# A two-block Trainium2 kernel: the second block's output gate, branch gates and branch projections in pairs of column tiles, seven half-size products for each pair

## What is computed

```python
proj = h @ w_in
(q_att, c_kv, q_idx, k_idx, w_idx, qkv, a, b, z, gates) = jnp.split(proj, SPLITS, axis=-1)
y_att = dsa_attention(...)
o = chunk_gated_delta_rule(...)                       # 8 heads of 128
y_dn = rms_norm_2(o, norm_g) * silu(z)
gates = sigmoid(gates)
g_att, g_dn = gates[..., :1024], gates[..., 1024:]
merged = g_att * (y_att @ w_br_att) + g_dn * (y_dn @ w_br_dn)
return merged @ w_out
```

## Time and profile before

| | us |
|---|---|
| median of 3 runs | 2307.83 |
| lowest and highest | 2305.79, 2315.35 |
| the profiled execution, its own time | 2306.49 |
| its span in the profile | 2304.8 |
| PE busy | 2222.1 |
| DVE busy | 901.3 |
| ACT busy | 469.4 |
| POOL busy | 114.3 |
| mean granted TensorE clock | 0.984 |

### The profile page before, as it was taken

The page is one execution under the profiler, slowest core; times in us unless marked ns, Lnnn a source line. Parts: engine busy times, 40 slices in busy tenths (PEclk is TensorE's granted clock), DMA queues, the critical chain, the costliest instruction groups (busy, mean ns, idle before and its releaser), DMA issues.

```text
span 2304.8 us, 22750 instructions
## 1 busy us (share of the span) xinstructions
PE 2222.1 (96%) x8731; PEld 1247.6 (54%) x8731; DVE 901.3 (39%) x1693; ACT 469.4 (20%) x984; POOL 114.3 (5%) x210
## 2 busy tenths in 40 slices
PE   8999999999999999999899999999999899999997
PEld 3447444468888444544656569444445544454443
DVE  3685532168887101185525755110015311111115
ACT  2134020112222001124535445100000100000002
POOL 0000000000000000000011000000000100000001
PEclk9999999999999999999999999999999899999999
DMA  4245222325555222112121110622241699999997
GB/s 158 73 162 194 73 73 73 119 88 178 184 172 183 55 73 91 57 55 81 42 78 55 58 52 1 249 105 79 73 145 55 258 428 427 428 425 427 427 428 300
DMA packets 45390, 385.23 MB, mean 167 GB/s; under 512 B 7066, under 2 KB 7194, under 8 KB 18650
## 3 DMA queue, kind: packets, MB, share of 16 engines
q1 hardware_dynamic: 30816, 317.39, 34.6%
q0 software_dynamic: 14176, 49.06, 6.2%
q10 hardware_dynamic: 289, 17.30, 2.2%
HBM read 369.54 MB, written 35.68 MB: 176 GB/s over the span
## 4 chain that ended last, share of the span: by engine, by line
PE 86%; DVE 5%; DMA 3%; issue 3%; ACT 1%; DVEq 1%; POOL 0%; SPq 0%; ACTq 0%; POOLq 0%
PE banks L591 22%; PE banks L1351 20%; PE banks L493 11%; PE banks L2605 8%; PE banks L2732 5%; PE banks L2618 4%; PE banks L1467 3%; PE banks L1590 2%; DMA arena<-in_experts 2%; DMA ring<-in_experts 1%; PE banks L600 1%; PE banks L646 1%; PE banks L662 1%; DVE arena L2072 1%; PE banks L653 1%
## 5 line engine op out<-in xcount | busy, mean ns | idle before, releaser
L1351 PE MATMUL banks<-arena,ring 128*128 128x512 f32 x1296 | 563.9, 595 | 0.0
L591 PE MATMUL banks<-arena,ring 128*128 128x512 f32 x1184 | 514.4, 595 | 5.9 <-DVE arena L1063 3.3
L1351 PEld LDWEIGHTS banks<-arena,ring 128*128 128x128 f32 x1296 | 245.7, 191 | 302.0 <-issue 300.5
L591 PEld LDWEIGHTS banks<-arena,ring 128*128 128x128 f32 x1184 | 225.7, 191 | 291.2 <-issue 283.2
L493 PE MATMUL banks<-ring 128*128 128x256 f32 x672 | 161.0, 389 | 8.0 <-DVE ring L463 3.9
L1657 ACT ACTIVATE arena<-banks 128x512 f32<-128x512 f32 (+4 forms) x151 | 78.5, 532 | 392.2 <-PE banks L1351 320.4
L493 PEld LDWEIGHTS banks<-ring 128*128 128x128 f32 x672 | 130.7, 195 | 27.8 <-DVE ring L463 4.3
L2732 PEld LDWEIGHTS banks<-arena 128*128 128x128 f32 x1024 | 121.0, 198 | 30.2 <-issue 28.9
L2732 PE MATMUL banks<-arena 128*128 128x128 f32 x1024 | 126.9, 284 | 5.7 <-issue 4.5
L2605 PE MATMUL banks<-ring,arena 128*64 128x512 f32 x528 | 120.1, 603 | 4.6 <-DMA ring<-in_experts 3.1
L493 PE MATMUL banks<-arena,ring 128*128 128x256 f32 x504 | 119.6, 380 | 0.0
(11 more groups left out here) (372 smaller groups left out, 1990.1 us busy)
## 6 DMA issues: line engine op xcount, KB each, us to landing
ring<-in_stream SPq DMA_DIRECT2D x105, 1024.0 KB, 4.8
arena<-in_experts SPq DMA_DIRECT2D x52, 2048.0 KB, 24.3
ring<-in_experts SPq DMA_DIRECT2D x44, 2048.0 KB, 21.9
arena<-in_w_adaT POOLq DMA_DIRECT2D x48, 512.0 KB, 4.7
expert_results<-arena POOLq DMA_DIRECT2D x60, 128.0 KB, 7.4
arena<-modulation_rows POOLq DMA_DIRECT2D x5, 512.0 KB, 9.8
arena<-in_xT SPq DMA_DIRECT2D x2, 1024.0 KB, 6.3
first_result<-arena POOLq DMA_DIRECT2D x4, 512.0 KB, 2.9
```

Source lines behind the costliest of these rows:

```text
L591: m = pe.matmul(bank, c.weight(at + k), rhs(k), start=k == 0, stop=k == tiles - 1)
L1351: m = pe.matmul(bank, c.weight(at + k), rhs(k), start=k == 0, stop=k == tiles - 1)
```

## The change

The 40 gemms `z`, `ga`, `gd`, `ba` and `bd` become 20 pairs in `pairs_pe`: four of `z`, eight of (`ga` t, `gd` t), four of `ba`, four of `bd`. `Halves` now carries its rows, its row sums and the count of `moving_sums` that it waits for, since three sets of rows are in use (h, the turned attention result, the delta result). The sums of h go to the fourth quarter of `ring` at the start of the second block's DVE program; those of the attention result to `BA_` during pair 9; those of the delta result to the fourth quarter of `ring` during pair 13. `moving_sums` counts each of its four instructions. Delta results are scaled in pairs 0 to 3 and turned, two jobs at a time, behind the closing of pairs 4 to 7. `ga` is kept in the `V_` region and `gd` in `BA_` + 4096, all eight tiles of each. Two of the three loads of `first_experts` (parts 0 and 1 of expert 0, whose places are the third and fourth quarter of `ring`) move behind the last `bd`. POOL's load of the first block's result waits for the last `ba` in place of the last `oT`. The `rank` job of the router gets bank 6.

```diff
-def moving_sums(c, v, rows):
+def moving_sums(c, v, rows, mixed):
...
+    v.tensor_tensor(t1, b12, b11, ALU.subtract).then_inc(c.sem("moving_sums"), 1)
+    v.tensor_tensor(t3, b22, b12, ALU.subtract).then_inc(c.sem("moving_sums"), 1)
...
 def pair_second(c, pe, h):
     pe.wait_ge(c.sem("pair_seeded"), h.n + 1)
+    pe.wait_ge(c.sem("moving_sums"), h.sums + 3)
...
 def pair_closes(c, pe, h):
     pe.wait_ge(c.sem("pair_lower"), h.n + 1)
+    pe.wait_ge(c.sem("moving_sums"), h.sums + 4)
...
+MIX_PAIRS = [(("z", 2 * i), ("z", 2 * i + 1)) for i in range(DH // 2)] \
+    + [(("ga", i), ("gd", i)) for i in range(DT)] \
+    + [((n, 2 * i), (n, 2 * i + 1)) for n in ("ba", "bd") for i in range(DT // 2)]
+SCALES_O, TURNS_O, MIXES_Y, MIXES_O = range(0, 4), range(4, 8), 9, 13
+
+def turns_o(j):
+    return (2 * (j - TURNS_O[0]), 2 * (j - TURNS_O[0]) + 1) if j in TURNS_O else ()
+
+def mix_pairs(c, h_sums):
+    h, yT, q = (c.view(at, DT, S) for at in (H_, K_, Q_))
+    sources = {"z": (h, c.mixed(), h_sums), "ga": (h, c.mixed(), h_sums),
+               "ba": (yT, c.mixed(BA_), h_sums + 4), "bd": (q, c.mixed(), h_sums + 8)}
+    return [Halves(c, a, b, *sources[a[0]]) for a, b in MIX_PAIRS]
...
 # plan_second
+    p.rotation((6, 7), (0, 2, 4))
+    for j, ((a, i), (b, k)) in enumerate(MIX_PAIRS):
+        p.pair((a, i, MIXERS[a][0]), (b, k, MIXERS[b][0]), [...])
+        for t in turns_o(j):
+            p.job("oT", t, "dve")
...
 # second_pe
-    for hd in range(DH):
-        gemm("z", hd, lambda k: h[:, k, :], DT)
-    for b in range(2 * TT):
-        pe.wait_ge(c.sem("o_scaled"), b + 1)
-        each("oT", b, lambda o, j, hd: pe.transpose(o, q[:, hd, ts(b)], c.ident[:, :]))
-    for t in range(DT):
-        gemm("ga", t, ...)
-        gemm("ba", t, ...)
-        gemm("gd", t, ...)
-        gemm("bd", t, ...)
+    def turn_o(j):
+        if j == MIXES_Y:
+            pe.wait_ge(c.sem("y_back"), 16)
+        for b in turns_o(j):
+            pe.wait_ge(c.sem("o_scaled"), b + 1)
+            each("oT", b, lambda o, j, hd: pe.transpose(o, q[:, hd, ts(b)], c.ident[:, :]))
+    pairs_pe(c, pe, mix_pairs(c, SECOND_SUMS), closed=turn_o)
...
 # second_act
+    pair_seeds(c, a, mixes[0])
     a.wait_ge(c.sem("powers"), 4)
     a.activation(sm[:, SO_S:SO_S + 32], sm[:, SO_S:SO_S + 32], ACT.Sqrt).then_inc(sem("powers_back"), 1)
+    for j, h in enumerate(mixes):
+        if j:
+            activated(mixes[j - 1].second)
+        if j + 1 < len(mixes):
+            pair_seeds(c, a, mixes[j + 1])
+        activated(h.first)
...
 # second_dve, at its start
+    v.wait_ge(c.sem("h"), DT)
+    moving_sums(c, v, h, c.mixed())
...
 # second_dve, behind the delta rule
+    weight_sums(c, v, mixes[0].n)
+    weight_sums(c, v, mixes[1].n)
     v.wait_ge(*c.put_away("o", 2 * TT - 1))
     v.scalar_tensor_tensor(power, ...).then_inc(sem("powers"), 1)
...
+    for j, p in enumerate(mixes):
+        pair_upper(c, v, p)
+        if j:
+            gated(mixes[j - 1].second)
+            for b in turns_o(j - 1):
+                turned_o(b)
+        pair_lower(c, v, p)
+        gated(p.first)
+        if j + 2 < len(mixes):
+            weight_sums(c, v, mixes[j + 2].n)
+        if j == SCALES_O[0]:
+            v.wait_ge(c.sem("powers_back"), 4)
+            v.reciprocal(power, power)
+            v.drain()
+        if j in SCALES_O:
+            scale_o(2 * j)
+            scale_o(2 * j + 1)
+        if j == MIXES_Y:
+            v.drain()
+            v.wait_ge(c.sem("y_back"), 16)
+            moving_sums(c, v, c.view(K_, DT, S), c.mixed(BA_))
+        if j == MIXES_O:
+            v.drain()
+            v.wait_ge(*c.finished("gd", DT - 1))
+            moving_sums(c, v, q, c.mixed())
+    gated(mixes[-1].second)
...
 # second_pool
-    g.wait_ge(*c.put_away("oT", 2 * TT - 1))
+    g.wait_ge(*c.finished("ba", DT - 1))
     g.dma_start(c.view(XTOK_, TT, D), c.x_spill).then_inc(c.sem("x_back"), 16)
...
 def first_experts(c, sp):
     load_expert(c, sp, 1, 1)
-    for i in range(2):
-        load_expert(c, sp, 0, i)
...
 # experts_sp
     sp.wait_ge(*c.finished("ba", DT - 1))
     load(2, 0)
+    sp.wait_ge(*c.finished("bd", DT - 1))
+    load(0, 0)
+    load(0, 1)
     sp.wait_ge(*c.put_away("bd", DT - 1))
     load(1, 2)
```

More of the change, by code:

```diff
@@ L47 @@
 MEAN_AT = 3
+SECOND_SUMS = 4
 class Plan:
@@ L478, with __init__ @@
 class Halves:
-    def __init__(self, c, first, second):
+    def __init__(self, c, first, second, rows, mixed, sums):
         self.c, self.first, self.second = c, first, second
@@ L484, in __init__ @@
         self.at = c.plan.pair_at[self.n]
+        self.rows, self.mixed, self.sums = rows, mixed, sums
         a, b = c.bank(*first), c.bank(*second)
@@ L492, in pair_product, with pair_opens @@
     for k in range(4):
-        m = pe.matmul(out, weights[:, k * P:(k + 1) * P], moving(k), start=first and k == 0, stop=k == 3,
+        m = pe.matmul(out, weights[:, k * P:(k + 1) * P], moving[:, k, :], start=first and k == 0, stop=k == 3,
                       skip_group_check=True)
     return m
-def pair_opens(c, pe, h, rows, sums, fresh):
+def pair_opens(c, pe, h, fresh):
     for name, i in (h.first, h.second):
@@ L543, in pairs_pe, with up_pairs @@
         if j + 1 < len(pairs):
-            pair_opens(c, pe, pairs[j + 1], rows, sums, j + 1 < fresh)
-        pair_third(c, pe, h, rows)
+            pair_opens(c, pe, pairs[j + 1], j + 1 < fresh)
+        pair_third(c, pe, h)
     pair_closes(c, pe, pairs[-1])
     closed(len(pairs) - 1)
+def up_pairs(c):
+    return [Halves(c, ("fg", t), ("fu", t), c.view(H_, DT, S), c.mixed(), 0) for t in range(1, FT)]
 def pair_seeds(c, a, h):
@@ L696, in first_pe @@
     gemm("fu", 0, lambda k: h[:, k, :], DT, ready="h2", since=DT)
-    pairs_pe(c, pe, [(("fg", t), ("fu", t)) for t in range(1, FT)], lambda k: h[:, k, :], 1)
+    pairs_pe(c, pe, up_pairs(c))
     pe.wait_ge(c.sem("act"), FT)
@@ L854, in first_act @@
     gate_silu(0)
-    ups = [Halves(c, ("fg", t), ("fu", t)) for t in range(1, FT)]
+    ups = up_pairs(c)
     pair_seeds(c, a, ups[0])
@@ L1253, in plan_second @@
             merge_64(ahead)
-    for h in range(DH):
-        p.job("z", h, "act", column_blocks(w, D, span(C_Z + h * P)))
-    for b in range(2 * TT):
-        p.job("oT", b, "dve")
-    for t in range(DT):
[L1259 to L1262, removed]
+    p.rotation((6, 7), (0, 2, 4))
+    for j, ((a, i), (b, k)) in enumerate(MIX_PAIRS):
+        p.pair((a, i, MIXERS[a][0]), (b, k, MIXERS[b][0]),
+               [column_blocks(MIXERS[n][1], D, span(MIXERS[n][2] + t * P)) for n, t in ((a, i), (b, k))])
+        for t in turns_o(j):
+            p.job("oT", t, "dve")
+    p.rotation(range(BANKS))
     p.align(CHUNK)
@@ L1276, in plan_second @@
     p.job("rt", TT - 1, "act")
-    p.job("rank", 0, "dve")
+    p.job("rank", 0, "dve", bank=RANK_BANK)
 B0 = 8192
@@ L2181, in second_dve, with gated @@
                                zt[:, g0:g0 + 4, t * P:(t + 1) * P], ALU.mult, ALU.mult) \
             .then_inc(c.emptied("dve", "oT", b), 1)
[L2183 to L2195, removed]
+    def gated(key):
+        name, t = key
+        if name == "ba":
+            v.wait_ge(*c.put_away("ga", t))
+            v.wait_ge(*c.finished("ba", t))
+            v.tensor_tensor(mg[:, t, :], c.bank("ba", t), mg[:, t, :], ALU.mult).then_inc(c.emptied("dve", "ba", t), 1)
+        if name == "bd":
+            v.wait_ge(*c.put_away("gd", t))
+            v.wait_ge(*c.finished("bd", t))
+            v.tensor_tensor(gate[:, t, :], c.bank("bd", t), gate[:, t, :], ALU.mult)
+            v.drain()
+            v.tensor_tensor(mg[:, t, :], mg[:, t, :], gate[:, t, :], ALU.add).then_inc(c.emptied("dve", "bd", t), 1)
@@ L2580 @@
 GU_BANK, Y_BANK, T_BANK, H_BANK = 0, 2, 4, 6
+RANK_BANK = H_BANK
 assert GR_ + 512 <= ARENA
```

87 lines of the change are left out of this document (36 added, 51 removed).

## The result

| | time, us | runs |
|---|---|---|
| before | 2306.81 (2304.16 to 2315.35) | 4 |
| after | 2282.39 (2279.23 to 2290.55) | 4 |

After takes 0.9896 of the time of before [0.9875, 0.9917]: 24.4 us less. The forecast was 2279.3 with 2274 to 2288; it was 3.1 us too low. The profiled execution of after is the slowest of its four, 2290.55 with a span of 2288.8. So its stretches are compared one by one, and not its end with the end of before.

The account below looks back on a forecast made before the run. PE, busy 96% of the span, was taken to bound the kernel. The stage's 241.7 + 0.6 + 3.5 + 3.3 + 0.6 = 249.7 us against 278.2 saves 28.5, giving 2279.3 against the median; 8 in 10: 2274 to 2288.

Parts of the forecast that it names:

- Products: The stage's 20 pairs take 12.087 us each instead of 13.735: 241.7 us in all, 33.0 saved.
- Fills: First three pairs each open with a bf16 product of 512 columns: 0.6 us for three.
- Transposes: The same 32 transposes, now in four parts within the stage: 3.5 us, at most 0.75 more four times.
- The opening, idle: Stage's first pair: PE idles 2.2 us for DVE's weight sums, then 0.75 for ACT's copies; 3.3 us lost in all.
- The opening, clock: Behind the opening's idle the clock holds, chance 0.58, range 2275 to 2284; rival: it falls, chance 0.27, 2284.0 us.
- The rival's price of 4.7: Clock falls at the opening, two to three products slow in full: 3.8 to 5.7 us, 4.7 taken; chance 0.27.
- The range: Whole kernel, 8 in 10: 2274 us (no opening loss beyond 2 us) to 2288.
- The slower rival: Clock swings inside the pairs at PE's short pauses; a fifth of the stage slow gives 2328 us; chance 0.03.
- Row sums, 14th pair: DVE's row sums meet a `ba` tile at pair 13: 11.0 us against 10.4, so 0.6 lost, between 0 and 2.
- DVE, ACT, SP, POOL: Other DVE and ACT work in the stage, SP's moved loads and POOL's later load: hidden, no cost.
- The end, and does it reach the end: Wait before wo2 unchanged; the expert stream starts 28.5 us earlier, equally long, so the saving reaches the kernel's end.
- The rival of the withheld gain: Expert stream doesn't move in full as early loads share the queues: 0 to 28.5 us kept back, 2300; chance 0.04.

Follow-up runs that it names:

- its two repetitions: The changed kernel measured again without edits: 2282.34 us, ratio 0.9906; and once more beside a later version: 2282.45 us, ratio 0.9893.
- half loads: Changed kernel with each expert load from expert 3 on bringing only the first half of its columns; one run, 2272.92 us.
- late loads: Changed kernel with the loads of parts 0 and 1 of expert 0 behind wo2 instead of the last bd; one run, 2282.95 us.
- the first block's opening: Changed kernel with the first block's weight sums moved around its row sums and ACT's first two copies ahead of the first Silu: 2276.32 us, ratio 0.9879.
- two experiments: Changed kernel with ten more fills in the opening's idle, 2281.75 us; changed kernel with first pair's weight sums ahead of the last two state updates, 2276.63 us.
- the run in which wo2 came 15.5 us earlier still: Changed kernel with the first block's opening reordered and the delta rule's last state update left out: 2266.69 us, ratio 0.9834.
- the control: The changed kernel measured again without edits, its profile the yardstick for the other versions: 2282.34 us, ratio 0.9906.
- the filled opening: Changed kernel with ten more bf16 fills ahead of the first pair's first product, in place of the idle: 2281.75 us, ratio 0.9898.
- the version without the last state: Changed kernel without the delta rule's last key transposes and state updates, which nothing reads: 2277.5 us, ratio 0.9887; profiled execution 2268.07.

## Why the prediction was right, and where it was off

- *Products.* 12.087 a pair forecast, 12.09 measured, four in a row in 48.35. Right. The products alone save 33.0 us; all that stands below takes 7.8 of it back.
- *Fills.* 0.2 each (1448.07 to 1448.29). Right.
- *Transposes.* Four groups, 0.87 each and no wait: 3.5. Right.
- *The opening, idle.* 2.2 and 0.75 forecast, 2.26 and 0.75 measured, released by the lines named. Right.
- *The opening, clock.* **This is the step that was off.** I took the clock to hold, with 0.58 against 0.27 for its fall. It fell in all six profiles that have this idle (after, its two repetitions, half loads, late loads, the first block's opening) and in none of the five in which it is filled or gone. Its cause is shown by the run that fills the idle and changes nothing else. Price by two experiments 2.93 and 3.19, by the rows 0.92 + 1.89 + 0.36 = 3.17. The rival's price of 4.7 was too high, since I let two to three products run slow in full, as in the first block; here the fall came about a microsecond after PE's restart, inside the second product. With the fall at 3.1 the sum gives 2282.4, and 2282.39 was measured. So close a hit is luck: the sum started from before's median of three runs, 2307.83, and with the fourth it was 2306.81. By stretches, 28.5 were forecast and 25.2 measured for the stage.
- *The range.* It held the result since it reached over the rival's 2284. Its lower bound has no working: an opening loss of 2 us in place of 3.3 gives 2278, not 2274. (The slower rival's sum, 2279.3 + 48, is 2327.3.)
- *Row sums, 14th pair.* 0.6 forecast, 0.38 measured. The delay on DVE was all there; PE's slack was a bit larger.
- *DVE, ACT, SP, POOL.* No cost, as forecast: no wait for them in 230 us of the stage but the 0.38.
- *The end, and does it reach the end.* 1.62 us before wo2, as before; 585.9 after wo2 against 585.6. Right. The rival of the withheld gain falls with the run in which wo2 came 15.5 us earlier still than in the control (1679.05 against 1694.59) and its distance to the end did not grow.
- *The slower rival.* A clock of 1.00 over 58 and 138 us of pairs refutes it here. The Trainium skill ("TensorE: Matmul & The Clock Gate", section "A second HAM failure mode: psum-queue depth-cycling") tells of a clock that swings where TensorE idles shortly between groups of bf16 products; it did not show in the pairs of any profile here, which are fp32 products. Each fall named in this document stands behind one idle stretch of 2.19 us or more.

What I should have read: against the fall I had one row, 157.2 to 159.4. For it I had 742.8, and another that I quoted for something else: in the earlier trace rows the 16 records behind a wait of 2.43 us took 5.35, where the next 16 of the same form took 3.65 (before, PE's timeline):

```profile
2268.48 3.65 PE L2605 MATMUL banks<-arena 128*64 128x512 f32 x16
```

The whole trace of before says more. Apart from the program's start, PE stood idle for 2 us or more seven times at a clock of 1.00. Behind six of these stretches, 2.43, 3.03, 3.30, 3.46, 3.90 and 4.55 us long, the clock was 0.50 within 2 us; only behind the 2.19 it stayed. The opening's 2.2 lay nearest to the one exception, so the rows did not decide it, but 0.58 for "holds" was too much. Its price had to be taken from the place where it bites.

## What to carry to other kernels

A scheme that saves products but needs sums first pays at its opening, twice: with the idle of TensorE, and with the slower clock behind it, which here was larger (2.9 to 3.2 against 2.3 us). So put the sums of the first unit into an earlier stretch in which their engine waits, and count every opening; four pairs of `z` were worth 6.6 us with the sums in time and 1.1 as built. Where a profiled execution lies apart from the median, compare it by stretches with a row of each at the same work before blaming the change.

## What was not expected of the hardware

- *The clock's fall behind an idle is not decided by its length alone.* The same idle of 2.19 us at 160 in unchanged code left the clock at 1.00 in before and in nine profiles of versions with the change, and lowered it in two (after and the filled opening), at 8.1 us each. Idles of 2.43 to 2.50 ahead of the last expert lowered it in ten of eleven (16 records in 5.15 to 5.35), and in one not (3.65, the version without the last state). One of 3.3 near 740 was followed by a product of 3.78 us in ten profiles and of 3.49 in one, but of 1.99 in another, again the one without the last state. In most sets of runs the highest value lies 6 to 9 us over the median, and the mean granted clock of that execution is the lower one (0.979 against 0.982 in one set); which idle it was isn't known where no profile was taken. What decides it stays open.
- *A stop of PE that names no engine.* In mid-stream PE stood 4.55 to 5.28 us at a branch between experts ("issue") with the DMA engines full, and 2.30 with half the loads. With full loads it was 2.39 and 2.13 in the two versions without the last state, so the loads are not its only cause, if they are one. It was not traced further.
